# Value products of the retention mixer with both weight halves in one 512 wide product, its roots spread by one product a head, and the first scores ahead of the wait for the values

## The reference, cut to what matters

```python
u = rmsnorm(h, mix_norm[l])
proj = u @ w_in[l]
u_pool, q, k, v, g = jnp.split(proj, [512, 1024, 1536, 2048], axis=-1)
a = pool_mixer(u_pool, pool_w[l], pool_scale[l])
b = retention(q, k, v, g, ret_norm[l])
h = h + jnp.concatenate([a, b], axis=-1) @ w_out[l]
```

## Time and profile before

| | |
|---|---|
| median of 3 runs | 1614.9 us (1614.07 to 1618.32) |
| profiled execution, its own time | 1615.48 us |
| span in its trace | 1613.7 us |
| PE busy | 1598.7 us, 99% of the span |
| DVE, ACT, POOL busy | 843.4 us, 497.7 us, 119.8 us |
| mean granted TensorE clock | 0.996 |

### The profile page before, as it was taken

How to read it: one execution, slowest core, us unless ns; L and a number is a source line. 1 busy time by engine, 2 the same in 40 slices (tenths; PEclk the granted TensorE clock), 3 DMA queues, 4 the chain that set the end, 5 groups by cost and what they waited for, 6 DMA issues and landing times.

```text
span 1613.7 us, 19892 instructions
## 1 busy us (share of the span) xinstructions
PE 1598.7 (99%) x8095; PEld 1359.1 (84%) x8095; DVE 843.4 (52%) x1032; ACT 497.7 (31%) x571; POOL 119.8 (7%) x106
## 2 busy tenths in 40 slices
PE   8999999999999999999999999999999999999998
PEld 6899999888888888888888888888988888888887
DVE  5897754674334344584544444346457445444444
ACT  4553264532222233441221222321223212222222
POOL 0100000020000000000000003135006000000000
PEclk9999999999999999999999999999999999999999
DMA  9544511212222222322222223332212222222332
GB/s 384 183 167 157 209 53 53 79 61 96 104 104 80 90 88 89 113 85 109 80 102 104 79 84 104 99 144 105 79 53 78 105 104 83 99 104 67 96 98 79
DMA packets 30361, 171.38 MB, mean 106 GB/s; under 512 B 3168, under 2 KB 5472, under 8 KB 16608
## 3 DMA queue, kind: packets, MB, share of 16 engines
q1 hardware_dynamic: 25952, 153.80, 27.3%
q0 software_dynamic: 4352, 16.78, 3.1%
HBM read 168.47 MB, written 2.10 MB: 106 GB/s over the span
## 4 chain that ended last, share of the span: by engine, by line
PE 96%; DMA 2%; DVE 1%; issue 0%; SPq 0%; ACT 0%; POOL 0%; POOLq 0%; DVEq 0%
PE bank L503 95%; DMA mod_w<-in_mod 2%; DVE mod_sum L1629 0%; PE bank L803 0%; SPq L346 0%; PE bank L747 0%; ACT w_hi L1193 0%; PE bank L1072 0%; PE bank L693 0%; SPq L349 0%; DVE y_ffn L2405 0%; ACT tmp L1396 0%; POOL root L408 0%; POOLq L123 0%; DVE qd L1982 0%
## 5 line engine op out<-in xcount | busy, mean ns | idle before, releaser
L1608 DVE TENSOR_TENSOR w_lo<-w_raw,w_hi 128x2048 fp32r<-128x2048 f32 x142 | 327.8, 2308 | 378.1 <-ACT w_hi L1193 378.0
L503 PE MATMUL bank<-a_hi,w_hi 128*128 128x512 f32 x1245 | 486.8, 391 | 0.0
L503 PE MATMUL bank<-a_hi,w_lo 128*128 128x512 f32 x1245 | 484.5, 389 | 0.0
L503 PE MATMUL bank<-a_lo,w_hi 128*128 128x512 f32 x1245 | 484.5, 389 | 0.0
L1193 ACT ACTIVATE w_hi<-w_raw 128x2048 fp32r<-128x2048 f32 x144 | 275.5, 1913 | 556.3 <-PE bank L503 556.1
L503 PEld LDWEIGHTS bank<-a_hi,w_hi 128*128 128x128 f32 x1245 | 233.8, 188 | 49.9 <-issue 1.9
L503 PEld LDWEIGHTS bank<-a_hi,w_lo 128*128 128x128 f32 x1245 | 233.7, 188 | 48.8
L503 PEld LDWEIGHTS bank<-a_lo,w_hi 128*128 128x128 f32 x1245 | 233.8, 188 | 48.1 <-issue 0.5
L503 PE MATMUL bank<-g_hi,w_hi 128*128 128x512 f32 (+1 forms) x544 | 210.4, 387 | 0.0
L503 PE MATMUL bank<-g_lo,w_hi 128*128 128x512 f32 (+1 forms) x544 | 210.0, 386 | 0.0
L503 PE MATMUL bank<-g_hi,w_lo 128*128 128x512 f32 (+1 forms) x544 | 210.0, 386 | 0.0
(11 more groups left out here) (299 smaller groups left out, 1604.2 us busy)
## 6 DMA issues: line engine op xcount, KB each, us to landing
w_raw<-in_ffn_in SPq DMA_DIRECT2D x66, 1024.0 KB, 4.8
w_raw<-in_ffn_out SPq DMA_DIRECT2D x24, 768.0 KB, 4.2
mod_raw<-in_mod POOLq DMA_DIRECT2D x16, 1024.0 KB, 5.5
w_raw<-in_ffn_out SPq DMA_DIRECT2D x24, 640.0 KB, 3.9
w_raw<-in_gla_in SPq DMA_DIRECT2D x12, 1024.0 KB, 4.8
w_raw<-in_mix_in SPq DMA_DIRECT2D x10, 1024.0 KB, 4.9
mod_w<-in_mod SPq DMA_DIRECT2D x8, 1024.0 KB, 18.8
w_raw<-in_gla_out SPq DMA_DIRECT2D x4, 1024.0 KB, 4.7
```

The lines of the kernel that those rows point to most:

```text
L503: return pe.matmul(out, lhs, rhs, start=first, stop=last, skip_group_check=True)
L1608: V.tensor_tensor(flat(w_lo[s]), flat(w_raw[s]), flat(w_hi[s]).bitcast(F32), ALU.subtract).then_inc(lo_done[s], 1)
```

## The change

Four edits, all in the mixer.

1. `w_hi[s]` and `w_lo[s]` become the two halves of one tensor `w_two[s]`. A new helper `tile_of_tokens` makes a value tile of 8 x 2 products: one 512 wide product streams both halves past `a_hi` (upper half to columns 0 to 255 of the bank, lower half to columns 256 to 511), and one 256 wide product streams `w_hi` past `a_lo` into columns 256 to 511. A tile now fills a whole bank.
2. Two banks a unit serve four tiles in turn, so tiles 2 and 3 wait until tiles 0 and 1 have been read (`free[b]`). ACT still copies columns 0 to 255; DVE adds columns 256 to 511, times the root, in a new step `values_added`, which frees the bank.
3. The wait for the copied values goes; `ret_scores_of(0)` stands ahead of a wait for the four banks.
4. The roots are spread by `broadcast`: DVE writes a diagonal of roots (128 x 512, one a head, `ret_diag` = `tmp`), and PE makes one full fp32 512 wide product with `ones` a head, two ahead of `mix_part(1, (3,))` and two behind it.

```diff
+        w_two = [place(f"w_two{s}", [P, 2, KD, UC], F32R) for s in range(2)]
+        w_hi, w_lo = ([w_two[s][:, j] for s in range(2)] for j in range(2))
...
+            def tile_of_tokens(b, s, t):
+
+                for k in range(KD):
+                    hi, lo = (x[:, k, t * P:(t + 1) * P] for x in (a_hi, a_lo))
+                    mm(bank[b][:].rearrange("p (w e) -> p w e", w=2), hi, w_two[s][:, :, k], k == 0, False)
+                    m = mm(bank[b][:, UC:2 * UC], lo, w_hi[s][:, k], False, k == KD - 1)
+                return m
...
             for n in range(2):
                 pe.wait_ge(lo_done[n], cnt.next(lo_done[n]))
                 pe.wait_ge(roped, cnt.upto(roped, CPU * (n + 3)))
-                for b in (2 * n, 2 * n + 1):
-                    for j in range(2):
-                        t = 2 * (b % 2) + j
-                        for k in range(KD):
-                            m = mm3(bank[b][:, j * UC:(j + 1) * UC],
-                                    (a_hi[:, k, t * P:(t + 1) * P], a_lo[:, k, t * P:(t + 1) * P]),
-                                    (w_hi[n][:, k], w_lo[n][:, k]), k == 0, k == KD - 1)
-                    m.then_inc(ready[b], 1)
+                for t in range(RCH):
+                    b = 2 * n + t % 2
+                    if t >= 2:
+                        pe.wait_ge(free[b], cnt.next(free[b]))
+                    tile_of_tokens(b, n, t).then_inc(ready[b], 1)
...
-            pe.wait_ge(v_copied, cnt.next(v_copied, 8))
             ret_scores_of(0)
+            for b in range(4):
+                pe.wait_ge(free[b], cnt.next(free[b]))
             gate_chunk(0)
...
-            pe.wait_ge(root_done, 12)
-            for h in range(HR):
-                for t in range(RCH):
-                    c = RCH * h + t
-                    m = mm(bank[4 + h][:, t * P:(t + 1) * P], root4[:, c:c + 1].to_broadcast([P, P]), ident[:], True, True)
-                m.then_inc(roots_ready, 1)
+            broadcast(4, T, ret_diag[0])
+            broadcast(5, T, ret_diag[1])
             mix_part(1, (3,))
+            broadcast(6, T, ret_diag[2])
+            broadcast(7, T, ret_diag[3])
...
@@ ACT @@
-                for b in (2 * n, 2 * n + 1):
+                for t in range(RCH):
+                    b = 2 * n + t % 2
                     act.wait_ge(ready[b], cnt.next(ready[b]))
-                    for j in range(2):
-                        t = 2 * (b % 2) + j
-                        nc.scalar.activation(vr[:, t, n * UC:(n + 1) * UC], bank[b][:, j * UC:(j + 1) * UC], ACT.Copy,
-                                             scale=root4[:, t:t + 1]).then_inc(v_copied, 1)
+                    nc.scalar.activation(vr[:, t, n * UC:(n + 1) * UC], bank[b][:, 0:UC], ACT.Copy,
+                                         scale=root4[:, t:t + 1]).then_inc(v_copied, 1)
                 split_hi(n)
...
@@ DVE @@
             rotate(5)
+
+            def values_added(n, tiles):
+
+                for t in tiles:
+                    x = vr[:, t, n * UC:(n + 1) * UC]
+                    b = 2 * n + t % 2
+                    dve.wait_ge(v_copied, cnt.next(v_copied))
+                    V.scalar_tensor_tensor(x, bank[b][:, UC:2 * UC], root4[:, t:t + 1], x, ALU.mult, ALU.add).then_inc(free[b], 1)
+
+            values_added(0, range(RCH))
             split_lo(0)
...
             ret_inputs(0)
+            values_added(1, (0, 1))
             ret_inputs(1)
+            values_added(1, (2, 3))
             split_lo(1)
...
+            for h in range(HR - 1):
+                diagonal(ret_diag[h], RCH, RCH * h)
             for h in range(HR):
                 dve.wait_ge(roots_ready, cnt.next(roots_ready))
                 V.tensor_tensor(gr[:, h], gr[:, h], bank[4 + h][:], ALU.mult).then_inc(scaled, 1)
-                if h:
+                if h == 0:
+                    diagonal(ret_diag[HR - 1], RCH, RCH * (HR - 1))
+                else:
                     head_lower(h - 1)
```

More of the change, by code:

```diff
@@ L150, in build @@
         w_raw = [place(f"w_raw{s}", [P, KD, UC]) for s in range(2)]
-        w_hi = [place(f"w_hi{s}", [P, KD, UC], F32R) for s in range(2)]
-        w_lo = [place(f"w_lo{s}", [P, KD, UC], F32R) for s in range(2)]
+        w_two = [place(f"w_two{s}", [P, 2, KD, UC], F32R) for s in range(2)]
+        w_hi, w_lo = ([w_two[s][:, j] for s in range(2)] for j in range(2))
         mod_at = top[0]
@@ L226, in build @@
         st = tmp[2]
+        ret_diag = tmp
         ret_q, ret_k, ret_p = ([tmp[j], dec_k[i]] for i, j in enumerate((0, 1, 3)))
```

## The result

| | before | changed |
|---|---|---|
| median | 1616.26 us (7 runs, 1614.07 to 1618.91) | 1622.49 us (7 runs, 1621.09 to 1624.90) |
| profiled execution, its own time | 1615.48 us | 1622.69 us |
| span | 1613.7 us | 1620.9 us |
| PE busy | 1598.7 us | 1601.3 us |
| mean granted clock | 0.996 | 0.994 |

The ratio is 1.0043, 95% interval [1.0034, 1.0052]: slower by 6.9 us (5.5 to 8.4). It is not the plain quotient of the two medians, which differ by 6.2 us. The forecast was +5.7. More runs of before moved its median up by 1.4 us from the 1614.9 that the forecast started from, so the predicted time of 1620.6 is 1.9 under the measured one, while the predicted difference is 1.2 short.

The account below looks back on a forecast made before the run. PE, busy 99%, was taken as the bound. Terms -0.84 + 5.25 + 0.96 - 1.14 give +4.2, roots 0.0, clock +1.5: +5.7 us over 1614.9, 1620.6 us; range 1618.3 to 1623.2, the forecast's own 1619.7 to 1621.6.

Parts of the forecast that it names:

- Rival 3: Ahead of unit 0's third value tile: bank 0 is free in time, PE is not held; 1613.9 us, chance 0.04.
- rival 4: Value products: bound by weight loads, not columns, a pair costing 0.227 us, 7.7 us less on PE; chance 0.03.
- Rival 1: Value stage: gaps as forecast but the clock holds; 1619.1 us, within 0.3%; chance 0.15.
- edit 1, wide product: Value tiles: a 512 plus a 256 wide product take 0.347 us instead of 0.360, over 64 pairs -0.84 us.
- edit 2, first gap: Ahead of unit 0's third tile: PE waits for DVE's addition behind the whole turn, +5.25 us.
- edit 2, second gap: Ahead of unit 1's third tile: PE waits for DVE's addition behind the splits and inputs of head 0, +0.96 us.
- edit 3, wait removed: Between values and scores: PE's wait for ACT's last copies goes, -1.14 us.
- new wait behind the scores: Ahead of the first gate product: the last addition is covered by the scores, with 0.04 us to spare, no cost.
- clock: Behind the first gap: PE's clock falls to its lower level, +1.5 us, bounded by nothing and 3.0.
- edit 4, roots: Root spreads: four products of 0.88 us replace 3.58 us, net 0.0 us, at most 0.1 either way.
- rival 2: Value stage: wide product gains nothing or clock stays down twice as long; 1621.4 to 1622.1 us, up to 1623; chance 0.12.
- the old fall: Kernel before, 697.67 to 701.01 us: eight steps at lowered clock lost 1.5 us, taken as the price of a fall.

Follow-up runs that it names:

- e1: The changed kernel with a bank of its own for each of the eight value tiles; ratio to before 0.9993, stage 24.05 us.
- e3: The changed kernel with DVE's additions of tiles 0 and 1 of unit 0 ahead of the turn; ratio to before 1.0009, stage 25.38 us.
- e7: The kernel before with one added wait: unit 0's third value tile waits for the turn's end; ratio to before 1.0048, stage 32.36 us.
- e2: The changed kernel with 22 small unread products filling the first gap on PE; ratio to before 1.0027, stage 30.11 us.
- e8: The changed kernel, unaltered, timed once more; ratio to before 1.0045, stage 32.82 us.
- e6: The changed kernel with unit 1's first two additions ahead of the inputs of head 0 on DVE; ratio to before 1.0040, stage 30.95 us.
- e9: The changed kernel with the additions of tiles 0 and 1 between the turn's two halves on DVE; ratio to before 1.0009, stage 28.63 us.
- e4: The kernel before with only the scores of head 0 moved ahead of the wait for copied values; ratio to before 1.0001, stage 24.28 us.
- e5: The kernel before with only the roots spread by diagonals and one product a head; ratio to before 1.0000, stage 25.49 us.

## Where the prediction held, and the step that failed

**Mechanism.** The forecast's chain held: PE stopped ahead of the third tile by the order of DVE, a fall of the clock behind it, a second short gap, a new wait met almost in time. e1 shows that the loss hangs on the banks, e3 that it hangs on DVE's order, e7 that a wait of about that length makes such a loss by itself, e2 that the clock is a part of it. Rival 3 (PE not held) and rival 4 (weight loads as the bound) are excluded by the trace: a pair takes 0.3475 to 0.353 at full clock, not 0.227. Rival 1 (the clock holds) did not come in any of the five profiled executions that have a gap of 2.1 us or more without a filler.

**Term by term**, for the stage of the first profile:

| term | predicted | measured |
|---|---|---|
| edit 1, wide product | -0.84 | -0.50 |
| edit 2, first gap | +5.25 | +5.02 |
| edit 2, second gap | +0.96 | +0.90 |
| edit 3, wait removed | -1.14 | -1.14 |
| new wait behind the scores | 0 | +0.13 |
| clock | +1.5 | +1.40 here, +2.9 in e8 |
| sum | +5.73 | +5.81 here, +7.33 in e8 |
| edit 4, roots | 0.0 | 0.0 (5.41 against 5.42) |

That the sum meets the first profile to 0.08 us is in part luck. The wide product saved 0.34 less and the new wait cost 0.13 more than forecast, the gaps came out 0.29 shorter and the clock 0.10 cheaper, and these cancel; and that execution happened to have the cheaper fall of the clock.

**The step that failed is the price of the clock.** It was taken from the fall at 697 us in the trace of before, 1.5 us, with 3.0 as an upper bound and as a part of rival 2 (chance 0.12). The runs show more than one price for the same gap, and most are higher: 1.4 us in the first profile, 2.2 in e6, 2.4 in e7, 2.9 in e8. In the first profile of the changed kernel, in e9 and in the old fall the clock was down for 3.4 us; in e6, e7 and e8 for 6.8. For the old fall these are the windows at its two ends, of the kernel before (697.3 to 700.7):

```profile
697.00:698.00 1.00, 1.00 (x8) 0.66 0.00 0
...
700.00:701.00 1.00, 1.00 (x4) 0.64 0.69 279
```

What a fall costs is half of that part of the low stretch in which PE has products: (1141.6 - 1138.7) / 2 = 1.4 in the first profile, (1147.4 - 1141.2) / 2 = 3.1 in e8 (2.9 measured), (1141.5 - 1136.9) / 2 = 2.3 in e6 (2.2), (1142.0 - 1136.9) / 2 = 2.6 in e7 (2.4). The Trainium skill, "TensorE: Matmul & The Clock Gate", section "Terms", gives a rule of the same form, the time at the lower level times one less the ratio. By the traces only the part with products counts: for the whole 6.8 us of e8 the rule would give 3.4, and 2.9 were lost. The Trainium skill's section "What's actually happening" says that the number of slow products at a kernel's start differs between runs of one kernel; these traces show the same behind a gap, about five slow pairs in the first profile and ten in e8. Over the four executions with a gap of 4.5 us or more (1.4, 2.2, 2.4, 2.9) the mean is 2.2, 0.7 over the term, which would have made the sum +6.4, inside the measured +5.5 to +8.4. The unprofiled executions say the same: by their lowest times the changed kernel (1621.09, 1621.24) is 7.0 to 7.3 us over before (1613.98 to 1614.07), and e2, where the clock stays up, 4.8 to 4.9, which leaves 2.2 to 2.4 us for the clock. That is an estimate, since two lowest executions need not be alike in all else. Why a fall lasts 3.4 us in one execution and 6.8 in the next stays open.

The old fall was also a poor model in kind: there PE was recorded busy for the whole of each us from 695 to 702, while in the changed kernel it stood still. (The lower edge of the forecast's own range, 1614.9 + 4.2 + 0.7, is 1619.8 and not 1619.7.)

**Edit 1** was over-sized. A pair takes 0.353 in tiles 0 and 1 (1128.06 to 1133.35 in 15 steps), not 0.347; over 64 pairs the changed kernel saves 0.50 us, and 0.23 net of the new wait in e1 against e4. The two runs of 256 in one operand are not the reason in every tile, for in the tiles between the two gaps the same pair takes 0.3475. Behind the second gap it is back at 0.353. Why it changes by 0.005 us stays open. **The gaps** were both a little over-sized: tiles 0 and 1 ended 0.10 later than reckoned, DVE's first addition started 0.08 before the turn's recorded end (1137.58 + 0.69), and PE started 0.06 after the addition's end, where 0.10 had been reckoned. **The new wait** was put at nothing with 0.04 of cover; the last addition, at 1158.62, ends at 1159.10, and PE starts the gate at 1159.36, 0.26 later, where I had reckoned 0.10 from release to start; by the 1.32 of before it would have started at 1159.23. In e4, where nothing holds the gate, the scores take 1.25 us (1149.89 to 1151.14), and against that the new wait is 0.20.

**What is not the change's.** The stage began 0.44 us later than before in the first profile and 2.94 in e8, from 1126.2 to 1130.6 over all executions. The traces show what goes with it: the clock falls in other places too, ahead of the stage, and not alike in each execution. Windows of PE around the two places, of the kernel before:

```profile
310.00:340.00 30.00, 29.90 (x167) 0.94 0.21 71
690.00:710.00 20.00, 19.67 (x99) 0.91 0.30 106
```

And of e8:

```profile
310.00:340.00 30.00, 29.92 (x160) 0.89 0.20 71
690.00:710.00 20.00, 19.67 (x91) 0.83 0.31 106
```

That is the lower level for 3.4 to 3.6 us at each place before, and for 6.6 to 6.8 in e8, whose stage began last. In e3 and e5, whose stages began first, the clock fell at the second place only; in e2, e6, e7 and e9 at the first only; in the first profile of the changed kernel at 22 us and at the second. The same shows in the unprofiled executions of before: those of 1614.0 to 1614.4 us have a mean granted clock of 0.997 to 0.998, those of 1618 us and more one of 0.994. So much of the spread between executions of one kernel goes with such falls, and a median of three moves with them. That they average out is assumed from the ratio, not shown. The last store's 0.8 us is seen in that one execution only.

## What to carry to other kernels

Where the engine that sets the time reuses a buffer, the release's place in the other engine's program order prices the change: here eight operations of an unrelated turn stood ahead of a 0.48 us addition. Ask first whether spare banks, or the addition moved ahead, remove the wait (e1 -7.25 us, e3 -5.92 us of the stage). A gap on TensorE costs its length and, for the gaps of 2.1 us and more here, a second amount for the clock, which differs between executions of one kernel (1.4 and 2.9 us for the changed kernel); put it in as a range, not as the one fall that a trace happens to show. Look at the granted clock of the whole trace, too, before a difference of a few us between two executions is put down to a change.

## What the hardware showed beyond what was expected

- The old fall and the five in the value stage left the clock down for 3.4 us (three) or 6.8 us (three); the same kernel with identical gaps had one of each. Falls elsewhere came in some executions of a kernel and not in others.
- Behind a gap of 2.1 us the clock fell, 0.8 us after it had ended, with PE at work (e9); a gap of 1.47 us (e3) and those of 0.9 us had no fall behind them. Each is from one or two executions.
- With products of the identity in the gap of 5.02 us the clock stayed at 1.00 (e2), though the gap's end did not move.
- A 512 product and a 256 product in turn step at 0.353 us ahead of the first gap and behind the second, and at 0.3475 between them, at a granted clock of 1.00 each time. With no gap (e1), or with the first filled (e2), they stay at 0.353.
